# Fourteen convolution tiles of the last block as pairs of 64-row products

## The chip, the cores and the metric

The kernel runs on one core of a Trainium2 chip. The metric is the device time of one execution in microseconds (us). Engines are called TensorE (PE in the rows, PEld its weight loads), VectorE (DVE), ScalarE (ACT), GpSimd (POOL) and SyncE (SP, which issues most transfers). TensorE's clock has two levels, 1.2 and 2.4 GHz; the profile gives the granted clock as a share of the higher.

## The reference

Three blocks over a sequence of 1024 tokens of width 1024. The first two (windowed and dilated attention, each with a gated feed-forward part) are not touched. The change is in the third:

```python
xn = rmsnorm_2(h, norm_gain[l])
proj = jnp.einsum('bld,dc->blc', xn, w_in[l])
u_ssm, z_ssm = proj[..., :512], proj[..., 512:1024]
h_conv, b_conv, c_conv, z_conv = four slices of 512 columns
y_ssm = s5_mixer(u_ssm, ...) * jax.nn.silu(z_ssm)
y_conv = short_conv_mixer(h_conv, b_conv, c_conv, conv_w[l]) * jax.nn.silu(z_conv)
h = h + jnp.einsum('blc,cd->bld', concatenate([y_ssm, y_conv]), w_out[l])
```

with `short_conv_mixer(h, b, c, w) = b * sum(w[k] * shifted(c * h, k) for k in range(3))`. Everything is float32.

## The kernel before

**Products in three parts.** A float32 product is made of three fp32r products: with a value split into a high part (rounded to fp32r) and a low part (the rest), it is high x high, high x low and low x high. The activations are `hT_high` and `h_low_mix`, 128 rows x 8 chunks (k) x 1024 tokens. A convolution tile `("conv", j, w)` is 128 output columns: j is the block of 128 channels, w says which of the four slices (0 and 1 are multiplied with each other, 2 is the gate in front, 3 goes through silu). It takes 8 chunks x 3 parts x 2 halves of 512 tokens = 48 products of 128 rows x 512 columns in `split_products` (L1437), accumulated in one of four accumulators `acc[0]` to `acc[3]`, each of two banks of PSUM (one for each half of the tokens).

**Tiles and their order.** `CONVS` is the order of the 16 tiles: (0,0), (0,1), (0,2), (1,0), (0,3), (1,1), (1,2), (1,3), (2,0), ... (3,3). The first two are made together in `first_convs`. The other fourteen follow one by one in `project_h` or `project_around`. In between stand three pieces of other work: after (0,2) the column statistics (L2082, 32 products of one column, `("stats",)`, behind waits on `sum_a` and `sum_b`); inside (1,0), after 5 chunks, `factor_spread` (L2056, 16 products, `("r spread",)`); inside (1,1), after 4 chunks, `turn_c` (L2065, 4 transposes, `("c^T",)`). All three write to `acc[3]`. Then TensorE waits for `powers_ready` from GpSimd and goes on with `z_with_lags`, whose lag products (L2090) have 64 rows and use alternating row halves.

**Accumulators.** `CONV_PLACES` gives the accumulator of a tile. `take` waits until the last user's result has been read (`acc_free`), and a tile's last product raises `acc_ready`. A ledger (`plan_accumulators`) counts the uses.

**Weights.** Three slots in turn hold the tiles. SyncE loads tile n (512 KB, L882) when TensorE has ended tile n-3; ScalarE makes the high half (L2560, `tile_highs`), VectorE the low half (L3681, `tile_lows`), and `tile_of` on TensorE waits for the low half (`tile_split`).

**VectorE's order** is written out by hand. At the stage's start: the sums of the norm (fifteen instructions, L3866 to L3875), the low half of (1,0); the small steps from the statistics to the factor (L3886 to L3898), with the low half of (0,3) among them; the copy of the spread factor (L3900); then for j = 0 to 3 the convolution: the product with tile 1 (L3918), the taps (L3920, L3921) with one of them on ScalarE (L2820), the product with tile 2 (L3924), the product of tile 3 with the factor (L3926), L3929, silu on ScalarE (L2825), L3933. The low halves are put in between: for j = 0 that of (1,1) behind L3924 and that of (1,2) behind L3933. Then come, for j = 0 alone, the two copies of C transposed (L3939, L3940). For j = 1 the product of (1,0) (L3915) is next, then the low half of (1,3). From there the same pattern goes on: behind the reading of a tile, the low half of one three or more places later.

**GpSimd** works out powers for the state-space part: eight steps that wait for nothing late, then eight that begin with the copies of C transposed, and then a memset (L1387) that raises `powers_ready`.

Of the kernel before, what the change touches and what calls it, by code (L numbers as in the profile page):

```python
# [11 lines left out]
P = 128  # L12
D = 1024
S = 1024
KC = D // P
ST = S // P
HALF = 512
DH = 64
# [12 lines left out]
TB = 8  # L31
# [81 lines left out]
HIGH_FREED = {"S3": ("P5", 1), "A11": ("P2", 1), "A22": ("P3", 1), "S2": ("P6", 1), "S1": ("P7", 0), "A12": ("P1", 0), "S4": ("P4", 0)}  # L113
TAIL_PLACES = (2, 0, 1, 3, 2, 0, 3, 1)
LAST_PLACES = (2, 0, 3, 1, 2, 3, 0, 3)
CONV_PLACES = ((2, 1, 0, 3), (2, 1, 0, 3), (0, 1, 2, 3), (0, 1, 2, 3))
KEPT = ("P7", "P1", "P6")
FIRST_KEPT = ("P1", "P7", "P6")
ADDED = ("Y0", "Y1", "X0")
# [37 lines left out]
CONVS = [(j, w) for j in range(4) for w in range(4)]  # L157
# [171 lines left out]
def two_blocks_kernel(nc, x, x_rows, c, ada_tiles, columns, ffn_w_in, ffn_w_out, a_tiles, a_w_out, a_sink,  # L329
# [3 lines left out]
    ACC, WTS = plan_accumulators(), plan_weights()  # L333

    ctx = ExitStack()
    with ctx:
# [3 lines left out]
        def sem(name):  # L340
            return ctx.enter_context(nc.semaphore(name))
# [311 lines left out]
        ssm_power = sem("ssm_power")  # L653
        ssm_exp = sem("ssm_exp")
        inv_ready = sem("inv_ready")
        c_ready = sem("c_ready")
        powers_ready = sem("powers_ready")
        lag_zero = sem("lag_zero")
        lag_ready = sem("lag_ready")
# [457 lines left out]
        def _(pool):  # L1117
# [261 lines left out]
            for i in range(TB - 2, -1, -1):  # L1379
                cmul(bpow[:, 0, :, i, :], bpow[:, 1, :, i, :], bpow[:, 0, :, i + 1, :], bpow[:, 1, :, i + 1, :], turns(a_r, GC), turns(a_i, GC))  # L1380

            pool.wait_ge(c_ready, 1)
            pool.wait_ge(acc_free[3], ACC[("c^T",)][2] + 1)
            for j in range(TB):
                cmul(cpow[:, 0, :, j + 1, :], cpow[:, 1, :, j + 1, :], cpow[:, 0, :, j, :], cpow[:, 1, :, j, :], turns(a_r, GC), turns(a_i, GC), minus=True)
# [22 lines left out]
        def _(pe):  # L1408
            def take(name):

                d, number, freed = ACC[name]
                if freed:
                    pe.wait_ge(acc_free[d], freed)
                return acc[d], acc_ready[d]
# [605 lines left out]
            def project_h(name, wait=None):  # L2020

                dst, ready = take(name)
                high, low = tile_of(name, KC)
                split_products(dst, range(KC), lambda k: high[:, k, :], lambda k: low[:, k, :], lambda k: hT_high[:, k, :],
                               lambda k: h_low_mix[:, k, :], wait).then_inc(ready, 1)

            def first_convs():

                places = [take(("conv", 0, w)) for w in range(2)]
                pe.wait_ge(down_added, direct_number(1, STEPS - 1, 4))  # L2030
                tiles = [tuple(tile_of(("conv", 0, w), KC)) for w in range(2)]
                for k in range(KC):
                    pe.wait_ge(h2_ready, k + 1)
                    for (dst, ready), (high, low) in zip(places, tiles):
                        mm = split_products(dst, [k], lambda k: high[:, k, :], lambda k: low[:, k, :], lambda k: hT_high[:, k, :],
                                            lambda k: h_low_mix[:, k, :], None, k == 0, k == KC - 1)
                        if k == KC - 1:
                            mm.then_inc(ready, 1)

            def project_around(name, before, between):  # L2040

                dst, ready = take(name)
                high, low = tile_of(name, KC)
                for chunks in (range(before), range(before, KC)):
                    mm = split_products(dst, chunks, lambda k: high[:, k, :], lambda k: low[:, k, :], lambda k: hT_high[:, k, :],
                                        lambda k: h_low_mix[:, k, :], None, chunks[0] == 0, chunks[-1] == KC - 1)
                    if chunks[0] == 0:
                        between()
                mm.then_inc(ready, 1)
# [9 lines left out]
            def turn_c():  # L2059
# [5 lines left out]
                        mm = nc.tensor.transpose(dst[:, 256 * r + P * n:256 * r + P * n + P], c_raw[:, r, n, :], ident[:, :])  # L2065
                mm.then_inc(ready, 1)

            first_convs()
            for j, n in CONVS[2:]:
                if (j, n) == (1, 0):  # L2070
                    project_around(("conv", j, n), 5, factor_spread)
                elif (j, n) == (1, 1):
                    project_around(("conv", j, n), 4, turn_c)
                else:
                    project_h(("conv", j, n))
                if (j, n) == (0, 2):
                    dst, ready = take(("stats",))
                    pe.wait_ge(sum_a, KC - 1)
                    pe.wait_ge(sum_b, KC)
                    for a, sq in enumerate((squares_a[:, 1, :], squares_b[:, 1, :])):  # L2080
                        for i in range(TB):
                            mm = nc.tensor.matmul(dst[:, TB * a + i:TB * a + i + 1], sq[:, P * i:P * i + P], ones[:, :], start=True, stop=True)  # L2082
                    mm.then_inc(ready, 1)

            pe.wait_ge(powers_ready, 1)
            def lag_pair(d, k, r):

# [839 lines left out]
        def _(dve):  # L2927
# [978 lines left out]
            for j in range(4):  # L3906
                def tap(k):
                    at = CONV_W + 4 * k + j
                    return vec[:, at:at + 1]

                if j == 0:
                    copied(("conv", 0, 0))
                    after(nc.vector.tensor_tensor(conv_y, conv_y, r_squared, ALU.mult))
                else:
                    nc.vector.tensor_tensor(conv_y, ready(("conv", j, 0)), r_squared, ALU.mult).then_inc(free(("conv", j, 0)), 1)  # L3915
                    tile_lows(LAST_SPLITS[4 * j + 3])
                    copied(("conv", j, 0))
                nc.vector.tensor_tensor(conv_v[:, 2:2 + S], conv_y, ready(("conv", j, 1)), ALU.mult).then_inc(free(("conv", j, 1)), 1)  # L3918
                dve.wait_ge(conv_tap, j + 1)
                after(nc.vector.scalar_tensor_tensor(conv_y, conv_v[:, 1:1 + S], tap(1), conv_y, ALU.mult, ALU.add))  # L3920
                after(nc.vector.scalar_tensor_tensor(conv_y, conv_v[:, 2:2 + S], tap(2), conv_y, ALU.mult, ALU.add))  # L3921
                if j:
                    tile_lows(LAST_SPLITS[4 * j + 4])
                nc.vector.tensor_tensor(conv_y, conv_y, ready(("conv", j, 2)), ALU.mult).then_inc(free(("conv", j, 2)), 1)  # L3924
                tile_lows(LAST_SPLITS[4 * j + 5])
                nc.vector.tensor_tensor(conv_v[:, 2:2 + S], ready(("conv", j, 3)), r_tile, ALU.mult).then_inc(acc_free[3], 1)  # L3926
                copied(("conv", j, 3))
                copied(("conv", j, 2))
                after(nc.vector.tensor_tensor(conv_y, conv_y, r_tile, ALU.mult))  # L3929
                dve.wait_ge(conv_silu, j + 1)  # L3930
                if j == 2:
                    dve.wait_ge(b_read, 1)
                nc.vector.tensor_tensor(y_conv[:, j, :], conv_y, conv_v[:, 2:2 + S], ALU.mult).then_inc(conv_ready, 1)  # L3933
                tile_lows(LAST_SPLITS[4 * j + 6])
                dve.wait_ge(conv_ready, j + 1)
                if j == 0:

                    c_rows = ready(("c^T",))[:, 0:512].rearrange("p (r c h) -> p r c h", r=2, c=NP)
                    nc.vector.tensor_copy(cpow[:, 0, :, 0, :], c_rows[:, 0]).then_inc(c_ready, 1)  # L3939
                    nc.vector.tensor_scalar(cpow[:, 1, :, 0, :], c_rows[:, 1], -1.0, None, ALU.mult).then_inc(acc_free[3], 1)  # L3940

            dve.wait_ge(conv_ready, 4)
# [195 lines left out]
```

## Time and profile before

| | |
|---|---|
| median of 3 runs | 2556.8 us (2555.84 to 2558.6) |
| the profiled execution | 2559.55 us |
| its span, first to last instruction | 2557.8 us |
| mean granted clock of TensorE | 0.997 |
| TensorE busy | 2519.9 us, 99% |
| VectorE busy | 1979.4 us, 77% |

All times in rows are from the span's start. A row of the timeline merges equal instructions that follow each other: start, length, engine, line, operation, output<-input, shape, count, and in brackets the idle time before it with what ended it. Products overlap in the array, so a row of n products is n-1 steps and one product's length long.

### The profile page before, as it was taken

To read this page: it belongs to the slowest core of one execution; us is meant where nothing else is said; L and a number is where in the kernel's file an instruction comes from. 1 tells how busy PE (TensorE), PEld (TensorE's weight loads), DVE (VectorE), ACT (ScalarE), POOL (GpSimd) and SP (SyncE) were. 2 spreads that over 40 slices of the span, in tenths; PEclk is the share of its full clock that TensorE was granted. 3 is DMA by queue.
4 is the path that set the end of the run, shared out by engine and by line. 5 is a ranking of instruction groups with operands and counts; after the bars stand their busy time and mean duration, and the time that the engine had idled before them with its cause. 6 is when DMAs were issued, how large, how long until landed. Compare 5 with 4: busy or idle time off the path is not lost.

```text
span 2557.8 us, 37284 instructions
## 1 busy us (share of the span) xinstructions
PE 2519.9 (99%) x12662; PEld 2042.5 (80%) x12662; DVE 1979.4 (77%) x3476; ACT 1071.7 (42%) x2010; POOL 318.0 (12%) x454
## 2 busy tenths in 40 slices
PE   8999999999999999999999999999999999999998
PEld 6777688888888888777776888888888888878987
DVE  7899848889998898845555898989999987443566
ACT  6666725433333333454445443333333342111233
POOL 2011101000000000201111200000000018971000
PEclk9999999999999999999999999999999999999999
DMA  6334231211112111222332111111112131113122
GB/s 240 121 135 141 100 91 58 65 59 49 53 53 62 53 53 53 105 69 91 99 108 92 50 50 46 59 60 49 53 57 62 49 101 57 50 42 60 34 99 83
DMA packets 182019, 192.62 MB, mean 75 GB/s; under 512 B 18354, under 2 KB 146578, under 8 KB 181491
## 3 DMA queue, kind: packets, MB, share of 16 engines
q1 hardware_dynamic: 169954, 147.48, 18.1%
q0 software_dynamic: 11952, 43.65, 5.5%
q8 instruction: 69, 1.13, 0.2%
q14 instruction: 44, 0.35, 0.0%
HBM read 177.34 MB, written 12.58 MB: 74 GB/s over the span
## 4 chain that ended last, share of the span: by engine, by line
PE 93%; DVE 3%; ACT 2%; issue 1%; DMA 0%; POOL 0%; SPq 0%; DVEq 0%
PE psum L1437 21%; PE psum L1759 10%; PE psum L1761 10%; PE psum L1760 10%; PE psum L1514 5%; PE psum L1811 4%; PE psum L1815 4%; PE psum L1812 4%; PE psum L1516 4%; PE psum L1515 4%; PE psum L1800 3%; PE psum L1645 3%; PE psum L1629 3%; PE psum L1614 1%; DVE arena L2955 1%; PE psum L1610 1%
## 5 line engine op out<-in xcount | busy, mean ns | idle before, releaser
L3244 DVE SCALAR_TENSOR_TENSOR xT<-psum,mod,xT 128x512 f32<-128x512 f32 x504 | 356.7, 747 | 61.5 <-PE psum L1815 61.2
L2375 ACT ACTIVATE w_high<-wpair 128x512 fp32r<-128x512 f32 x240 | 146.4, 626 | 315.7 <-DVE wpair L3176 244.5
L1437 PE MATMUL psum<-hT_high,w_low 128*128 128x512 f32 x928 | 263.1, 394 | 0.2 <-DVE arena L2951 0.2
L1437 PEld LDWEIGHTS psum<-hT_high,w_low 128*128 128x128 f32 x928 | 174.3, 189 | 38.6 <-issue 2.5
L1514 PE MATMUL psum<-hT_high,w_low 128*128 128x512 f32 x480 | 200.2, 417 | 3.4 <-DVE h_low_mix L3719 3.3
L2593 ACT ACTIVATE arena<-arena 128x256 f32<-128x256 f32 (+3 forms) x296 | 146.6, 498 | 118.3 <-DVE arena L3530 118.0
L1516 PE MATMUL psum<-hT_high,w_low 128*128 128x512 f32 x480 | 189.0, 394 | 0.0
L1515 PE MATMUL psum<-h_low_mix,w_low 128*128 128x512 f32 x480 | 188.6, 393 | 0.0
L1761 PE MATMUL psum<-hT_high,w_low 128*128 128x512 f32 x480 | 186.7, 389 | 0.0
L1759 PE MATMUL psum<-hT_high,w_high 128*128 128x512 f32 x472 | 183.6, 389 | 0.0
L1760 PE MATMUL psum<-h_low,w_high 128*128 128x512 f32 x472 | 183.6, 389 | 0.0
L3162 DVE TENSOR_TENSOR w_low<-wpair,w_high 128x512 fp32r<-128x512 f32 x240 | 162.2, 683 | 2.4 <-ACT w_high L2375 1.9
L3681 DVE TENSOR_TENSOR w_low<-wpair,w_low 128x1024 fp32r<-128x1024 f32 x70 | 89.4, 1278 | 88.9 <-ACT w_low L2560 88.6
L1237 POOL TENSOR_TENSOR w_high<-arena,w_high 128x512 fp32r<-128x512 f32 x2 | 2.6, 1290 | 1233.5 <-ACT w_high L2362 1233.5
L1811 PE MATMUL psum<-hT_high,w_low 128*128 128x512 f32 x360 | 140.0, 389 | 0.0
L1437 PE MATMUL psum<-h_low_mix,w_low 128*128 128x512 f32 x448 | 136.2, 393 | 0.2 <-ACT arena L2302 0.2
L2560 ACT ACTIVATE w_low<-wpair 128x1024 fp32r<-128x1024 f32 x76 | 80.0, 1054 | 130.1 <-DMA wpair<-in_w_in_dram 94.6
L1514 PEld LDWEIGHTS psum<-hT_high,w_low 128*128 128x128 f32 x480 | 90.3, 188 | 44.5 <-issue 24.7
L3530 DVE CUSTOM_DVE_ANT_0 arena<-psum,arena 128x192 f32<-128x192 f32 (+2 forms) x180 | 53.7, 353 | 86.6 <-PE psum L1614 86.6
L2421 ACT ACTIVATE arena<-psum 128x512 f32<-128x512 f32 x80 | 47.9, 599 | 169.9 <-PE psum L1761 114.3
L2614 ACT ACTIVATE arena<-psum 128x1024 f32<-128x1024 f32 (+2 forms) x80 | 85.4, 1067 | 75.5 <-PE psum L1629 75.1
L3176 DVE TENSOR_TENSOR wpair<-wpair 128x512 f32<-128x512 f32 x160 | 110.0, 688 | 6.6
(492 smaller groups left out, 6362.4 us busy)
## 6 DMA issues: line engine op xcount, KB each, us to landing
wpair<-in_ffn_w_in_dram SPq DMA_DIRECT2D x176, 256.0 KB, 2.9
wpair<-in_ada_tiles_dram POOLq DMA_DIRECT2D x20, 1024.0 KB, 5.3
arena<-in_ffn_w_out_dram SPq DMA_DIRECT2D x80, 256.0 KB, 2.9
wpair<-in_ada_tiles_dram POOLq DMA_DIRECT2D x32, 512.0 KB, 3.6
wpair<-in_w_in_dram SPq DMA_DIRECT2D x24, 512.0 KB, 3.8
wpair<-in_b_tiles_dram SPq DMA_DIRECT2D x18, 512.0 KB, 3.3
arena<-in_ada_tiles_dram SPq DMA_DIRECT2D x8, 1024.0 KB, 15.8
wpair<-in_a_tiles_dram SPq DMA_DIRECT2D x12, 512.0 KB, 5.1
```

The lines of the kernel that those rows point to most:

```text
L1437: mm = nc.tensor.matmul(dst[:, HALF * a:HALF * a + HALF], w(k), src(k)[:, HALF * t:HALF * t + HALF], start=first and n == 0 and w is high ...
L1514: nc.tensor.matmul(dst, high[:, k, :], hT_high[:, k, rows], start=k == 0, stop=False)
L1515: nc.tensor.matmul(dst, high[:, k, :], h_low_mix[:, k, rows], start=False, stop=False)
L1516: mm = nc.tensor.matmul(dst, low[:, k, :], hT_high[:, k, rows], start=False, stop=k == KC - 1)
L1759: nc.tensor.matmul(bank[dst], high[:, k, :], moving_high(k), start=start and k == 0, stop=False, skip_group_check=not start)
L1760: nc.tensor.matmul(bank[dst], high[:, k, :], moving_low(k), start=False, stop=False, skip_group_check=not start)
L1761: mm = nc.tensor.matmul(bank[dst], low[:, k, :], moving_high(k), start=False, stop=k == 3, skip_group_check=not start)
L1811: nc.tensor.matmul(dst, down_high[w][:, cols], hid_high[v], start=start, stop=False, skip_group_check=not start)
L2375: nc.scalar.activation(of_step(s, first_high, part_high)[name], part_raw[name], ACT.Copy).then_inc(part_high_ready, 1)
L2593: e = nc.scalar.activation(s, s, ACT.Exp, bias=stat_n[:, ti, h:h + 1], scale=-1.0, accum_out=stat_l[:, ti, h:h + 1])
L3162: nc.vector.tensor_tensor(part_low[name], part_raw[name], as_f32(high), ALU.subtract).then_inc(part_split, 1)
L3244: nc.vector.scalar_tensor_tensor(xT[:, m, rows], psum[:, HALF * j:HALF * j + HALF], mod[:, l, 40 + m:41 + m], xT[:, m, rows], ALU.mult, AL ...
```

## The change

Products of the fourteen tiles behind `first_convs` are cut into products of 64 rows. `by_rows` makes one pass over a tile: for each chunk and part, the upper 64 rows are multiplied for one half of the tokens and the lower 64 rows for the other half, so the two go to two banks. A second pass (`swapped`) exchanges the halves and adds what is missing. A pass is 24 such pairs. Two tiles are made together in `pair_of_tiles`: first pass of tile A, first pass of tile B, second pass of A (behind a wait on the new semaphore `rows_done`, raised by A's first pass), second pass of B (likewise). The pairs are (0,2) with (1,0), (0,3) with (1,1), (1,2) with (1,3), and so on. The column statistics stand behind the first passes of the first pair, `factor_spread` inside its last pass after 5 chunks, `turn_c` behind the first pass of (1,2). The places of the tiles of j = 2 and 3 are those of j = 0 and 1. `c_ready` goes, and `inv_ready` counts to 2 in its place. VectorE's, ScalarE's and SyncE's orders are otherwise as before.

```diff
-CONV_PLACES = ((2, 1, 0, 3), (2, 1, 0, 3), (0, 1, 2, 3), (0, 1, 2, 3))
+CONV_PLACES = ((2, 1, 0, 3), (2, 1, 0, 3), (2, 1, 0, 3), (2, 1, 0, 3))
...
-            pool.wait_ge(c_ready, 1)
+            pool.wait_ge(inv_ready, 2)
...
+            def by_rows(name, swapped, chunks=range(KC)):
+
+                d = ACC[name][0]
+                high, low = tile_of(name, KC)
+                for k in chunks:
+                    for w, srcs in ((high, (hT_high, h_low_mix)), (low, (hT_high,))):
+                        for s in srcs:
+                            first, last = k == 0 and w is high and s is hT_high, k == KC - 1 and w is low
+                            for row in (0, DH):
+                                half = int(row > 0) ^ int(swapped)
+                                at, rows = slice(HALF * half, HALF * half + HALF), slice(row, row + DH)
+                                mm = nc.tensor.matmul(acc[d][:, at], w[rows, k, :], s[rows, k, at], start=first and not swapped, stop=last and swapped)
+                if KC - 1 in chunks:
+                    mm.then_inc(acc_ready[d] if swapped else rows_done, 1)
+
+            def pair_of_tiles(i, names, behind_first=None, behind_firsts=None, inside_last=None):
+
+                take(names[0])
+                by_rows(names[0], False)
+                if behind_first:
+                    behind_first()
+                take(names[1])
+                by_rows(names[1], False)
+                if behind_firsts:
+                    behind_firsts()
+                pe.wait_ge(rows_done, 2 * i + 1)
+                by_rows(names[0], True)
+                pe.wait_ge(rows_done, 2 * i + 2)
+                by_rows(names[1], True, range(5))
+                if inside_last:
+                    inside_last()
+                by_rows(names[1], True, range(5, KC))
...
             first_convs()
-            for j, n in CONVS[2:]:
-                if (j, n) == (1, 0):
-                    project_around(("conv", j, n), 5, factor_spread)
-                elif (j, n) == (1, 1):
-                    project_around(("conv", j, n), 4, turn_c)
-                else:
-                    project_h(("conv", j, n))
-                if (j, n) == (0, 2):
...
+            pairs = [[("conv", j, w) for j, w in CONVS[n:n + 2]] for n in range(2, 16, 2)]
+            pair_of_tiles(0, pairs[0], None, column_statistics, factor_spread)
+            pair_of_tiles(1, pairs[1])
+            pair_of_tiles(2, pairs[2], turn_c)
+            for i in range(3, 7):
+                pair_of_tiles(i, pairs[i])
             pe.wait_ge(powers_ready, 1)
...
-                    nc.vector.tensor_copy(cpow[:, 0, :, 0, :], c_rows[:, 0]).then_inc(c_ready, 1)
+                    nc.vector.tensor_copy(cpow[:, 0, :, 0, :], c_rows[:, 0]).then_inc(inv_ready, 1)
```

## Rows read from the trace of the kernel before

**Rows 1.** The page: span, busy times, clock by slices, chain that ended last.
```profile
span 2557.8 us, 37284 instructions
...
PE 2519.9 (99%) x12662; PEld 2042.5 (80%) x12662; DVE 1979.4 (77%) x3476; ACT 1071.7 (42%) x2010; POOL 318.0 (12%) x454
...
PEclk9999999999999999999999999999999999999999
...
PE 93%; DVE 3%; ACT 2%; issue 1%; DMA 0%; POOL 0%; SPq 0%; DVEq 0%
```

**Rows 2.** The chain from 2120 to 2290: start, us, what, count.
```profile
2119.94 17.91 PE psum L1437 x79
2137.84 3.82 PE psum L2082 x32
2141.66 9.76 PE psum L1437 x30
2151.43 1.78 PE psum L2056 x16
2153.21 20.44 PE psum L1437 x90
```

**Rows 3.** Windows: length, busy time and count by engine, granted clock, DMA.
```profile
core 0: us, PE busy (x) PEld busy (x) DVE busy (x) ACT busy (x) POOL busy (x), PEclk, DMA share, GB/s
...
2141.50:2147.60 6.10, 6.10 (x15) 4.79 (x16) 3.72 (x17) 0.42 (x2) 4.80 (x17) 0.50 0.00 0
...
27.90:31.30 3.40, 3.40 (x10) 2.62 (x9) 3.37 (x7) 0.82 (x2) 0.00 (x0) 0.51 1.02 408
```

**Rows 4.** TensorE's timeline, ahead of the second of these windows.
```profile
27.01 0.50 PE L1514 MATMUL psum<-hT_high,w_low 128*128 128x512 f32 x1 [2.55 <-DVE h_low_mix L3719]
```

**Rows 5.** TensorE's timeline: plain fp32 products, of 64 and of 128 rows.
```profile
1127.03 1.13 PE L1614 MATMUL psum<-arena 64*128 64x256 f32 x8
...
2423.49 3.73 PE L2178 MATMUL psum<-arena,hT 128*128 128x128 f32 x32
...
2441.03 3.98 PE L2187 MATMUL psum<-arena 64*128 64x128 f32 x64
```

**Rows 6.** TensorE's timeline around the first lag products.
```profile
2289.13 0.61 PE L1437 MATMUL psum<-hT_high,w_low 128*128 128x512 f32 x2
2289.67 0.61 PE L2090 MATMUL psum<-arena 64*16 64x128 f32 x8
2290.22 0.73 PE L1437 MATMUL psum<-hT_high,w_low 128*128 128x512 f32 x2
```

**Rows 7.** VectorE's timeline, from the norm's sums to tile (1,2).
```profile
2133.95 2.03 DVE L3873 TENSOR_TENSOR arena<-arena 128x1024 f32<-128x1024 f32 x1
2135.82 1.22 DVE L3681 TENSOR_TENSOR w_low<-wpair,w_low 128x1024 fp32r<-128x1024 f32 x1
...
2146.01 0.17 DVE L3898 TENSOR_TENSOR r_token<-rst 128x8 f32<-128x8 f32 x1
...
2153.25 2.19 DVE L3900 COPY arena<-psum 128x1024 f32<-128x1024 f32 x1 [7.08 <-PE psum L2056]
...
2164.38 1.56 DVE L3681 TENSOR_TENSOR w_low<-wpair,w_low 128x1024 fp32r<-128x1024 f32 x1
2168.25 1.23 DVE L3926 TENSOR_TENSOR arena<-psum,arena 128x1024 f32<-128x1024 f32 x1 [2.30 <-PE psum L1437]
...
2172.43 1.64 DVE L3681 TENSOR_TENSOR w_low<-wpair,w_low 128x1024 fp32r<-128x1024 f32 x1
```

**Rows 8.** The copies of C, what follows them on VectorE; GpSimd's last step.
```profile
2174.20 0.42 DVE L3939 COPY arena<-psum 128x256 f32<-128x256 f32 x1
...
2176.00 1.22 DVE L3681 TENSOR_TENSOR w_low<-wpair,w_low 128x1024 fp32r<-128x1024 f32 x1
...
2243.79 0.11 POOL L1387 MEMSET arena<- 128x16 f32 x1
```

**Rows 9.** VectorE's timeline from a tile's end to the next split; the load.
```profile
2190.50 1.22 DVE L3924 TENSOR_TENSOR arena<-arena,psum 128x1024 f32<-128x1024 f32 x1 [3.95 <-PE psum L1437]
2195.31 1.56 DVE L3681 TENSOR_TENSOR w_low<-wpair,w_low 128x1024 fp32r<-128x1024 f32 x1 [3.58 <-ACT w_low L2560]
...
wpair<-in_w_in_dram SPq DMA_DIRECT2D x11, 512.0 KB, 3.8
```

More of the change, by code:

```diff
@@ L655, in two_blocks_kernel @@
         inv_ready = sem("inv_ready")
-        c_ready = sem("c_ready")
+        rows_done = sem("rows_done")
         powers_ready = sem("powers_ready")
@@ L2066, in turn_c @@
                 mm.then_inc(ready, 1)
-            first_convs()
-            for j, n in CONVS[2:]:
-                if (j, n) == (1, 0):
-                    project_around(("conv", j, n), 5, factor_spread)
-                elif (j, n) == (1, 1):
-                    project_around(("conv", j, n), 4, turn_c)
-                else:
-                    project_h(("conv", j, n))
-                if (j, n) == (0, 2):
[L2077 to L2083, printed above, removed]
+            def by_rows(name, swapped, chunks=range(KC)):
[11 more added lines that the diff above has]
+                    mm.then_inc(acc_ready[d] if swapped else rows_done, 1)
@@ new lines, in column_statistics @@
+            def column_statistics():
+                dst, ready = take(("stats",))
+                pe.wait_ge(sum_a, KC - 1)
+                pe.wait_ge(sum_b, KC)
+                for a, sq in enumerate((squares_a[:, 1, :], squares_b[:, 1, :])):
+                    for i in range(TB):
+                        mm = nc.tensor.matmul(dst[:, TB * a + i:TB * a + i + 1], sq[:, P * i:P * i + P], ones[:, :], start=True, stop=True)
+                mm.then_inc(ready, 1)
+            first_convs()
+            pairs = [[("conv", j, w) for j, w in CONVS[n:n + 2]] for n in range(2, 16, 2)]
```

## The prediction

> **What bounds the kernel now.** I read the page first. TensorE is busy 2519.9 of 2557.8 us and carries 93% of the chain that ended last; its granted clock is at the higher level (2.4 GHz) in nearly every slice [rows 1]. So the program ends when TensorE's queue has been worked off, and a change of this stage is worth what it adds to or takes from that queue. The chain over the stage shows the stage's make-up: 79, 30 and 90 products in a row, broken only by the column statistics and the spread of a factor, with no wait of TensorE between them [rows 2]. The last of these pieces gives the rate: 20.44 us for 90 products of 128x512 is 0.2271 us each; I use 0.2267, which the single timeline steps repeat. The tile (0,2) begins 48 products before the statistics, at 2137.68 - 48 x 0.2267 = 2126.80.
>
> Next the windows, for the clock. The statistics are 32 products of one column, 3.8 us [rows 2]; just after them the granted clock is 0.50 for 6.1 us, that is 1.2 GHz [rows 3]. There 30 products take 9.76 us [rows 2] instead of 6.8: 3.0 us lost. A second place shows the same after real idleness: TensorE waits 2.55 us [rows 4] and the next 3.4 us run at 0.51 [rows 3], 1.7 us lost. An idle stretch of a few us on TensorE thus costs itself and a further 1.7 to 3.0 us.
>
> Last the DVE queue, in order of time, because DVE makes the low half of each weight tile (L3681), and TensorE can't start a tile before it.
>
> **The change, part by part.**
>
> *Products.* 14 tiles x 48 = 672 full products become 672 pairs of 64-row products, each pair into two banks. The trace has 64-row products in alternating row halves and banks, but in plain fp32, whose columns take twice as long. Attention's, 256 columns (8 in 1.13 us, the first lasting 0.48): three further pairs in 0.65 us, 0.217 a pair [rows 5], for what is 512 column times, 0.2133 us at 2.4 GHz; some 3 ns on top. The full fp32r product has 13.4 ns on top of the same 0.2133. With 128 columns, 64 products of 64 rows take 3.98 us, 0.124 a pair with the first one's latency in it and 0.117 without, against 3.73/32 = 0.117 for a full 128-row product [rows 5]. So pairs do run side by side, at least level with a full product. Bounds for a pair here: 0.216 and 0.2267. I take 0.216, as attention's rows are the nearest in stream length (512 column times a pair) and way of issue: 672 x 0.0107 = -7.2 us. At the other end the gain is nothing.
>
> *Changes between 128-row and 64-row products.* Around the lag products, the step 2289.36 to 2289.67 is 0.31 instead of 0.23, and 2289.67 to 2290.22 is 0.55 for four pairs of 0.11: some 0.2 us for a way in and out [rows 6]. The stage has four such: the whole, and the statistics, spread and turn of C inside it. +0.8 us. The Trainium skill, "TensorEngine Tiling (Array Packing)", Key Properties, says that a change of tiling mode drains the engine; these rows agree.
>
> *First stall: tile (1,0).* Before, TensorE wants it after all 48 products of (0,2) and after the statistics, past 2141. Now its first pass comes after 24 pairs, at 2126.8 + 0.1 + 24 x 0.216 = 2132.1. Its low half is the DVE instruction at 2135.82, ended 2137.04 [rows 7], behind the fifteen sums of the norm, which DVE has worked through without a gap; nothing of them moves. Stall 5.0 us.
>
> *Second stall: tile (1,1).* Its low half lies on DVE behind a chain that begins with the spread of the factor: from 2153.25 to 2164.38 + 1.56 = 2165.94, 12.7 us [rows 7]. Before, TensorE had 18 products of (1,0) and 48 of (0,3) left after the spread, 15.0 us: the tile was ready 2.3 us before it was wanted. Now it has 9 pairs of (1,0) and one pass of 24 of (0,3): 7.1 us, plus some 0.4 for the bank of (0,3), which the copy of 2.19 us frees [rows 7]. Stall 12.7 - 7.1 - 0.4 = 5.2, and 0.4 before it. The factor itself isn't late: its last step stands 4.5 us behind the statistics' end [rows 7], and 39 pairs lie between.
>
> *Third: tile (1,2).* DVE takes (0,3) at 2168.25, when TensorE ends it, and has the low half of (1,2) at 2172.43 + 1.64 = 2174.07 [rows 7], 5.8 us. Between the end of (0,3) and the start of (1,2) there is now one pass, 5.2 us. Stall 0.6, with semaphore steps 0.8.
>
> *Fourth: C transposed.* The transposes move from inside (1,1) to behind the first pass of (1,2). DVE waits for them in its fixed order, and behind that wait stand the two copies, the product of (1,0) and the low half of (1,3): 2174.20 to 2177.22, 3.0 us [rows 8]. TensorE needs that low half for its very next pass. With the transposes' own latency: stall 3.4 us. GpSimd, which waits for the same copies, has its powers ready at 2243.79 [rows 8], 44 us before TensorE asks for them (the next stage begins six products before 2289.67 [rows 6], at 2288.2); the 24 us that C comes late are covered. The new semaphore count (2 in place of a semaphore of its own) costs nothing.
>
> *From the fourth pair on.* A slot freed by the first of a pair must be filled again within two passes, 10.4 us. The row pattern gives 2190.50 (tile done) to 2195.31 + 1.56 = 2196.87 (split done), 6.4 us, the load's 3.8 us in it [rows 9]: no stall, 4 us to spare. The bank orders leave each bank at least a pass to be read. The waits on rows_done look at a pass that ended a whole pass earlier: nothing.
>
> *Clock.* The first, second and fourth stall are longer than the 2.55 us after which the clock fell [rows 3, 4]. Each costs 1.7 to 3.0 us; I take 2.4, three times, +7.0 us. The statistics cost their 3.0 us before and after. The Trainium skill, "TensorE: Matmul & The Clock Gate", HAM oscillation, also has idle gaps of a few us bring the lower clock back; the rows agree.
>
> **Sum.** Stalls 5.0 + 0.4 + 5.2 + 0.8 + 3.4 = 14.8; clock 7.0; switches 0.8; pairs -7.2: +15.4 us. The profiled execution took 2559.55 us (span 2557.8), so 2575.0 for it. It stands 2.75 above the median of the three runs, 2556.8; against the median 2572.2. Predicted: 2572 us.
>
> **Rivals.**
> (a) A pair costs what the full product costs, 0.2267, as the rows with 128 columns say [rows 5]; against it stands attention's 3 ns. The stalls hardly change (4.7 the first), so +22.6: 2579.4. The Trainium skill, "TensorEngine Tiling (Array Packing)", Overview, promises gain from row tiling only where the contracted dimension is small; here it is a whole 128, and by that rule this is the case.
> (b) The pair is slower than a full product: the two weight changes are paid one after the other, 0.2133 + 2 x 0.0134 = 0.240 us, +9.0 instead of -7.2: 2588. If the two products did not overlap at all, 0.43 us a pair, it would be some 140 us more; the 64-row rows speak against that.
> (c) The stalls come, but the clock stays up after them, since each is soon followed by dense products: +8.4, 2565.2. Against it: the fall after 2.55 us.
> (d) Not slower. Mechanism: the pairs stream faster than one column a cycle and row half. To pay 14.8 + 7.0 + 0.8 = 22.6 us, 672 pairs must each save 33.6 ns, so it decides at 0.193 us a pair. That is under the 0.2133 that 512 columns need, and no row shows it.
>
> **How the numbers follow.** Forecast 0.50, (a) 0.27, (b) 0.08, (c) 0.11, (d) 0.04. The range: from (c), 2565, to (a) with 3.0 us of clock at each stall, 2556.8 + 14.8 + 9.0 + 0.8 = 2581.4, rounded up for pairs a little above 0.2267: 2564 to 2583. It leaves out (b) and (d), 12 in 100. The runs before lie within 0.1% of each other, so 0.2% (5 us) is about what can be told from no change. Faster: only (d), of which half, 0.02; same the other half, 0.02; slower 0.96.
>
> **What would show it.** TensorE idle some 5 us from about 2132, released by DVE L3681; again some 5 us in the middle of the pair (0,3), (1,1); 3 to 4 us behind the transposes of C; granted clock at 0.5 after each. Starts of pairs 0.216 apart (0.227 for (a), 0.240 for (b)). From the fourth pair on no idleness. The stage, 2126.8 to 2288.2 before, ends near 2304. It would be wrong if DVE came to the low half of (1,0) before 2132, or if the pair's rate were not between 0.216 and 0.227.

## The result and the profile after

The changed kernel takes 2583.14 us (median of four runs, 2582.84 to 2583.51), the kernel before 2557.7 (2555.84 to 2558.96): 1.0% slower, ratio 1.0100, 95% interval 1.0087 to 1.0113. The forecast was 2572, with a range of 2564 to 2583: right in direction, too low by 11 us, and 0.14 us outside the range. The profiled executions are 2582.84 and 2559.55 us, 23.3 apart.

The page of the changed kernel, against [rows 1]:

```profile
span 2581.1 us, 38642 instructions
...
PE 2528.2 (98%) x13334; PEld 2063.4 (80%) x13334; DVE 1979.3 (77%) x3476; ACT 1073.1 (42%) x2010; POOL 314.0 (12%) x454
...
PEclk9999999999999999999999999999999998999999
```

TensorE has 672 product records more and is busy 8.3 us longer (a part of it at the lower clock); the other 15 of the 23.3 us are idle time. The chain through the stage, against [rows 2], shows where it went:

```profile
2136.23 1.06 DVE w_low L3714
...
2137.43 7.32 PE psum L2079 x47
2144.75 3.94 PE psum L2108 x32
2148.69 11.97 PE psum L2079 x73
2160.66 2.00 PE psum L2056 x16
...
2162.68 2.20 DVE arena L3933
...
2174.46 1.47 DVE w_low L3714
...
2176.07 14.02 PE psum L2079 x96
...
2194.31 1.70 DVE w_low L3714
...
2196.14 5.75 PE psum L2079 x48
2201.89 0.60 PE psum L2065 x4
...
2204.47 1.33 DVE w_low L3714
...
2205.94 105.27 PE psum L2079 x912
```

Before, this stretch of the chain was TensorE alone. Now it leaves TensorE four times for VectorE, and each time it comes back through L3714, the low half of a tile (L3681 before). The same four waits in TensorE's timeline, with the idle time in brackets:

```profile
2137.43 0.56 PE L2079 MATMUL psum<-hT_high,w_low 64*128 64x512 f32 x2 [4.33 <-DVE w_low L3714]
...
2176.07 0.80 PE L2079 MATMUL psum<-hT_high,w_low 64*128 64x512 f32 x2 [5.39 <-DVE w_low L3714]
...
2196.14 0.49 PE L2079 MATMUL psum<-hT_high,w_low 64*128 64x512 f32 x2 [0.63 <-DVE w_low L3714]
...
2205.94 0.77 PE L2079 MATMUL psum<-hT_high,w_low 64*128 64x512 f32 x2 [3.46 <-DVE w_low L3714]
```

They are the first passes of (1,0), (1,1), (1,2) and (1,3). A record lasts 0.39 us and the next would begin 0.227 after its start, so each costs 0.16 us more than its bracket: 4.5, 5.6, 0.8 and 3.6, together 14.5 us. Behind three of them the clock is down, as these windows show (granted clock is the first number behind POOL's):

```profile
2137.43:2144.70 7.27, 7.27 (x49) 6.25 (x49) 0.01 (x1) 0.00 (x0) 5.44 (x23) 0.77 0.01 2
...
2148.60:2154.80 6.20, 6.20 (x31) 4.88 (x33) 3.83 (x17) 0.42 (x2) 5.43 (x23) 0.50 0.00 0
2176.07:2182.10 6.03, 6.03 (x28) 5.22 (x30) 0.00 (x0) 0.00 (x0) 5.79 (x10) 0.50 0.00 0
...
2205.90:2209.40 3.50, 3.46 (x16) 3.25 (x18) 2.28 (x2) 2.10 (x2) 3.34 (x5) 0.51 0.03 5
2209.40:2311.00 101.60, 101.60 (x898) 98.64 (x894) 38.63 (x28) 13.73 (x13) 73.80 (x94) 1.00 0.17 48
```

The second is the statistics' own, as before. In the first the clock comes back up before the pass is over, so its mean is 0.77. From 2209.4 on TensorE is never idle and the clock is up, and a pair takes 0.2267 us from start to start (mean of 444 steps), which is the step of a full product. That is rival (a).

VectorE's side, against [rows 7] and [rows 8]: the low half of (1,0) is made when it was before, that of (1,1) 13.2 us behind the spread (12.7 before), and the copies of C wait 6.6 us for TensorE.

```profile
2136.07 1.21 DVE L3714 TENSOR_TENSOR w_low<-wpair,w_low 128x1024 fp32r<-128x1024 f32 x1
...
2162.68 2.19 DVE L3933 COPY arena<-psum 128x1024 f32<-128x1024 f32 x1 [9.37 <-PE psum L2056]
...
2174.38 1.54 DVE L3714 TENSOR_TENSOR w_low<-wpair,w_low 128x1024 fp32r<-128x1024 f32 x1
...
2202.58 0.42 DVE L3972 COPY arena<-psum 128x256 f32<-128x256 f32 x1 [6.59 <-PE psum L2065]
```

A measure for what follows: **the stage**, from the start of the last feed-forward product (L1800) to the start of the first lag product (L2090 before, L2123 after). It is 184.86 us before (2104.81 to 2289.67) and 207.47 after (2105.26 to 2312.73): +22.6. The part ahead of it differs by up to 3.7 us between executions in which nothing of it was changed (2104.8 to 2108.5), so single spans can't tell a microsecond here, and the stage can.

### The profile page after: what moved, and what is told of

Its sections match the earlier page's. It is cut to its first block, busy times and chain, and to the rows that moved or that the text cites. A ratio compares the mean times of both kernels' runs of the same rounds, so it can differ in the third digit from the quotient of the medians.

```text
span 2581.1 us, 38642 instructions
## 1 busy us (share of the span) xinstructions
PE 2528.2 (98%) x13334; PEld 2063.4 (80%) x13334; DVE 1979.3 (77%) x3476; ACT 1073.1 (42%) x2010; POOL 314.0 (12%) x454
## 3 DMA queue, kind: packets, MB, share of 16 engines
q1 hardware_dynamic: 169954, 147.48, 17.7%
## 4 chain that ended last, share of the span: by engine, by line
PE 91%; DVE 5%; ACT 2%; issue 1%; DMA 0%; POOL 0%; SPq 0%; DVEq 0%; ACTq 0%
PE psum L1437 14%; PE psum L1759 10%; PE psum L1760 10%; PE psum L1761 10%; PE psum L2079 6%; PE psum L1514 5%; PE psum L1812 4%; PE psum L1815 4%; PE psum L1811 4%; PE psum L1516 4%; PE psum L1515 4%; PE psum L1645 3%; PE psum L1629 3%; PE psum L1800 2%; PE psum L1614 1%; DVE arena L2988 1%
## 5 line engine op out<-in xcount | busy, mean ns | idle before, releaser
L1514 PE MATMUL psum<-hT_high,w_low 128*128 128x512 f32 x480 | 200.7, 418 | 3.0 <-DVE h_low_mix L3752 2.8
L1516 PE MATMUL psum<-hT_high,w_low 128*128 128x512 f32 x480 | 189.1, 394 | 0.0
L1515 PE MATMUL psum<-h_low_mix,w_low 128*128 128x512 f32 x480 | 188.8, 393 | 0.0
L1761 PE MATMUL psum<-hT_high,w_low 128*128 128x512 f32 x480 | 186.7, 389 | 0.0
L2079 PE MATMUL psum<-hT_high,w_low 64*128 64x512 f32 x896 | 152.8, 403 | 13.8 <-DVE w_low L3714 13.8
L3714 DVE TENSOR_TENSOR w_low<-wpair,w_low 128x1024 fp32r<-128x1024 f32 x70 | 89.0, 1272 | 83.3 <-ACT w_low L2593 83.0
L1437 PE MATMUL psum<-hT_high,w_low 128*128 128x512 f32 x480 | 140.8, 394 | 0.2 <-DVE arena L2984 0.2
L1811 PE MATMUL psum<-hT_high,w_low 128*128 128x512 f32 x360 | 140.1, 389 | 0.0
L1514 PEld LDWEIGHTS psum<-hT_high,w_low 128*128 128x128 f32 x480 | 90.6, 189 | 44.0 <-issue 24.7
L2079 PEld LDWEIGHTS psum<-hT_high,w_low 64*128 64x128 f32 x896 | 100.5, 194 | 23.4 <-issue 15.6
## 6 DMA issues: line engine op xcount, KB each, us to landing
arena<-in_ada_tiles_dram SPq DMA_DIRECT2D x8, 1024.0 KB, 15.6
```

The costliest lines, as they stand in the source:

```text
L1437: mm = nc.tensor.matmul(dst[:, HALF * a:HALF * a + HALF], w(k), src(k)[:, HALF * t:HALF * t + HALF], start=first and n == 0 and w is high ...
L1514: nc.tensor.matmul(dst, high[:, k, :], hT_high[:, k, rows], start=k == 0, stop=False)
L1515: nc.tensor.matmul(dst, high[:, k, :], h_low_mix[:, k, rows], start=False, stop=False)
L1516: mm = nc.tensor.matmul(dst, low[:, k, :], hT_high[:, k, rows], start=False, stop=k == KC - 1)
L1761: mm = nc.tensor.matmul(bank[dst], low[:, k, :], moving_high(k), start=False, stop=k == 3, skip_group_check=not start)
L1811: nc.tensor.matmul(dst, down_high[w][:, cols], hid_high[v], start=start, stop=False, skip_group_check=not start)
```

## The experiments

The theory: the pairs cost what full products cost, and the 22.6 us are three late low halves and a short fourth (14.5), the clock behind them, and under 1 us for changes between 128 and 64 rows. The rivals: 64-row products are themselves the slow part; or the stalls are one chain, where what one gives back another takes.

| kernel | median us | ratio (95%) | stage us | stage to before |
|---|---|---|---|---|
| changed | 2583.14 | 1.0100 (1.0087 to 1.0113) | 207.47 | +22.6 |
| e1, full products, new order | 2583.04 | 1.0092 (1.0077 to 1.0108) | 206.76 | +21.9 |
| e2, 64 rows, old order | 2567.02 | 1.0027 (1.0017 to 1.0038) | 189.69 | +4.8 |
| e3, three moves | 2562.47 | 1.001 (1.0001 to 1.0019) | 185.20 | +0.3 |
| e5, low half of (1,0) earlier | 2577.51 | 1.0067 (1.0053 to 1.008) | 199.63 | +14.8 |
| e6, low half of (1,1) earlier | 2577.18 | 1.0063 (1.0049 to 1.0076) | 198.85 | +14.0 |
| e7, C transposed earlier | 2578.03 | 1.007 (1.0056 to 1.0084) | 200.54 | +15.7 |
| e8, e3 with full products | 2559.87 | 1.0003 (0.9994 to 1.0012) | 184.56 | -0.3 |
| e9, statistics between products | 2559.42 | 0.9995 (0.9986 to 1.0004) | 182.48 | -2.4 |
| e10, stalls filled | 2576.64 | 1.0071 (1.0058 to 1.0085) | 200.42 | +15.6 |

The kernel before had medians of 2560.18 (beside e1 to e4), 2560.75 (e5, e6, e7, e9) and 2558.91 us (e8, e10); the ratios are to those. Each stage is read from one profiled execution. The expectations below give the distance from the kernel before without saying by which measure; where medians and stages disagree about them, the text says so.

### e1: full products in the new order

```diff
-                            for row in (0, DH):
-                                half = int(row > 0) ^ int(swapped)
-                                at, rows = slice(HALF * half, HALF * half + HALF), slice(row, row + DH)
-                                mm = nc.tensor.matmul(acc[d][:, at], w[rows, k, :], s[rows, k, at], ...)
+                            at = slice(HALF * int(swapped), HALF * int(swapped) + HALF)
+                            mm = nc.tensor.matmul(acc[d][:, at], w[:, k, :], s[:, k, at], start=first, stop=last)
```

> The order of the changed kernel (pairs of tiles, four passes, statistics, spread and turn where the change puts them), but each pass made of 24 full products of 128 rows for one half of the tokens. Theory (the time comes from the order: three late low halves and the clock behind them; a pair of 64-row products costs what one full product does): stalls of 4.5, 5.4, 0.6 and 3.5 us and the fallen clock stay; only the changes between 128 and 64 rows go, so 0.5 to 1.5 us below the changed kernel, 21 to 25 us above the kernel before, ratio 1.008 to 1.010. Rival (64-row products are what is slow): within 5 us of the kernel before.

21.9 of the 22.6 us stay without a single 64-row product in the fourteen tiles. The waits are those of the changed kernel, four for the low half and 0.2 us for the bank of (0,3):

```profile
PE psum L2077 <- DVE w_low L3712: 14.4, 4, 5.7
PE psum L2077 <- DVE arena L3931: 0.2, 1, 0.2
```

So the order is what costs. The difference left for the 64 rows is 0.7 us. It is what they add on balance: e1 waits longer, 14.4 us for low halves against 13.8 in the changed kernel, and 0.2 for the bank, which TensorE's waits in the changed kernel do not show. So a part of what the 64 rows cost is hidden behind waits that are there anyway; the rows themselves may cost up to 0.7 + 0.6 + 0.2 = 1.5 us, an estimate.

### e2: 64-row products in the old order

```diff
-            pairs = ...
-            pair_of_tiles(...)
+            for n in range(2, 16):      # one tile at a time
+                take(name); by_rows(name, False)
+                pe.wait_ge(rows_done, n - 1)
+                by_rows(name, True)
```

(The spread stands in the second pass of (1,0) after 2 chunks, C transposed between the passes of (1,1); the accumulators' places are those of before.)

> 64-row products in the order of the kernel before: one tile at a time, its first pass, the wait on rows_done, its second pass; statistics, spread and turn after as many products as before. Theory: no stall by a low half, the clock as before; 0.8 us for the changes between 128 and 64 rows, and at each of 14 swaps the wait for the first pass's last product, worked out at 0.25 us from a product's 0.39 us in the records against a step of 0.227: 3.5 us. 3 to 6 us above the kernel before, ratio 1.001 to 1.0025. Rival (64-row products are what is slow): 20 us or more above.

The stage is 4.8 us longer than before, in the forecast 3 to 6. The chain of the kernel, one tile to a row:

```profile
2199.36 11.22 PE psum L2079 x96
2210.58 0.04 issue
2210.62 11.22 PE psum L2079 x96
```

A tile takes 11.26 us against 48 x 0.2267 = 10.88: 0.38 for the wait at the swap, where I had worked out 0.25, and 14 x 0.38 = 5.3. That is what making two tiles together avoids, and it is less than what the order of the pairs cost. The stage met its forecast with help: behind the statistics the clock cost 1.85 us here and 2.9 in the kernel before (see e3), so at an equal clock the stage would be some 6 us longer, which is 5.3 and the 0.8 for changes of rows. The median is 6.8 us above before, ratio 1.0027, and that is a miss of the expected 3 to 6 us and 1.001 to 1.0025; the part ahead of the stage was 2.2 us longer in the profiled execution.

### e3: the three moves

```diff
 # VectorE, norm's sums
                 weighted(k, ...)
+                if k == KC - 2:
+                    tile_lows(LAST_SPLITS[3])
                 plain(k, ...)
 # VectorE, convolution, j == 0 (ScalarE's high half likewise ahead of its tap)
+                    tile_lows(LAST_SPLITS[5])
                 dve.wait_ge(conv_tap, j + 1)
 # TensorE
-            pair_of_tiles(1, pairs[1])
-            pair_of_tiles(2, pairs[2], turn_c)
+            pair_of_tiles(1, pairs[1], None, None, turn_c)
+            pair_of_tiles(2, pairs[2])
```

> The changed kernel with three moves: the low half of (1,0) put before the last but three of the norm's sums; the high and low half of (1,1) put before the first tap; C transposed inside the last pass of the second pair, after 5 chunks. Theory: the stalls of 4.5, 5.4 and 3.5 us and their clock (1.6, 2.8, 1.6 us) go, some 19.5 us; left over are the changes between 128 and 64 rows and stalls under 1 us each: 1 to 4 us above the kernel before, ratio 1.0003 to 1.0015. Rival (64-row products are what is slow): still 15 us or more above.

The stage is 22.3 us shorter than the changed kernel's and 0.3 us longer than before's, under the expected 1 to 4 us; the median is 2.3 us longer, within them. The chain stays on TensorE from end to end:

```profile
2129.21 11.15 PE psum L2079 x96
2140.36 3.66 PE psum L2108 x32
2144.02 10.69 PE psum L2079 x78
2154.71 1.98 PE psum L2056 x16
2156.69 2.30 PE psum L2079 x18
...
2159.00 20.01 PE psum L2079 x174
2179.01 0.59 PE psum L2065 x4
2179.60 111.13 PE psum L2079 x975
```

A part of this may not be the moves' doing: behind the statistics 39 pairs take 10.69 us, 1.85 more than their 8.84 at the higher clock, where the changed kernel loses 3.1 (11.97) and the kernel before 2.9. The loss is as small, 1.6 to 1.9 us, in e2, e5, e7, e8 and e10, but not in e1 (2.9) and e6 (2.65). e7 pays for it elsewhere: its first stall is there, and the pass behind that stall takes 8.34 us, against 7.32 in the changed kernel.

```profile
2139.76 8.34 PE psum L2079 x48
2148.10 3.66 PE psum L2108 x32
2151.76 10.69 PE psum L2079 x75
```

What sets how long the clock stays down is not settled. Some 1.3 us of e3's gain on the changed kernel, and 1.1 us of how well it compares with the kernel before, hang on it and are not shown to come from the moves.

### e5, e6, e7: each move alone

> The changed kernel with the low half of (1,0) alone put before the last but three of the norm's sums. Theory: each stall stands for itself and costs its idle time and half of the time at the fallen clock behind it; here 4.5 and 1.6 us go, the stalls before (1,1), (1,2) and (1,3) stay at 5.4, 0.6 and 3.5 us: 16 to 18 us above the kernel before, ratio 1.006 to 1.007. Rival (one chain: what the first stall gives back is lost again at the second): still 20 us or more above.

> The changed kernel with the high and low half of (1,1) alone put before the first tap. Theory: 5.4 us of stall and 2.8 us of clock go, less some 0.3 us: 14 to 16 us above the kernel before, ratio 1.0055 to 1.0065. Rival (the chain behind it, with one instruction more ahead of the taps, makes the wait before (1,2) longer and takes half of it back): 18 us or more above.

> The changed kernel with C transposed inside the last pass of the second pair, after 5 chunks, and nothing else. Theory: VectorE then has the copies behind it when it comes to (1,0) and the low half of (1,3) before TensorE asks; 3.5 us of stall and 1.6 us of clock go, 17 to 19 us above the kernel before, ratio 1.0065 to 1.0075. Rival (VectorE would be late with the low half of (1,3) anyway, as the slot of (0,3) is only then loaded anew): less than 2 us gained on the changed kernel.

Each is faster than the changed kernel by more than a wait: 7.8, 8.6 and 6.9 us of stage. Taken by the starts of passes in the traces, e5 gains 7.7 us up to the spread, 1.5 of them at the statistics and behind them; e6 gains 8.3 around (1,1) and nothing at the statistics, whose own 32 records take 0.5 us longer while the pairs behind them lose 0.5 less; e7 gains 6.6 from (1,1) on. Elsewhere each differs from the changed kernel by 0.6 us at most. The three pieces add up to 22.6, and e3 gained 22.3: the stalls add up. The rival of one chain falls. So does that of e7, where VectorE was said to be late anyway. e7's 6.6 are its stall of 3.5, its clock of 1.6, the wait before (1,2) of 0.8, which went with it, and 0.5 less clock lost behind the stall of (1,1), for which no cause is shown.

The ratios came out as expected in all three. The medians are 16.8, 16.4 and 17.3 us above before, the second 0.4 over its range. The stages, at +14.8, +14.0 and +15.7, are 1.2 and 1.3 us under the ranges of e5 and e7, and at the lower end of that of e6. e5's other three waits stand as they were:

```profile
PE psum L2079 <- DVE w_low L3714: 9.4, 3, 5.0
```

### e8: the moves with full products

The edit is e1's and e3's together.

> The three moves of e3 and full products in place of 64-row pairs, in the new order. Theory: against e3 only the changes between 128 and 64 rows go, 0.7 us as between the changed kernel and e1; level with the kernel before, ratio 1.000, the stage within 1 us of before's 184.9 us from the last feed-forward product to the first lag product. Rival (the new order costs something of its own besides the three stalls): 2 us or more above the kernel before in the stage.

0.6 us below e3 in the stage and 0.3 below before, as expected. That does not make the new order free. The clock behind the statistics costs 1.6 us here and 2.9 in the kernel before, so at an equal clock e8 would be some 1 us above. TensorE's waits show where a part of it lies, in the bank of (0,3) and the low half of (1,2):

```profile
PE psum L2077 <- DVE w_low L3711: 0.4, 1, 0.4
PE psum L2077 <- DVE arena L3931: 0.2, 1, 0.2
```

e3 has no such wait, so the 0.6 us between e3 and e8, as the 0.7 between the changed kernel and e1, is what 64 rows cost on balance, and not all that they cost.

### e10: stalls filled with products that nobody uses

```diff
-                take(names[1])
+                dst, _ = take(names[1])
+                if i < 3:
+                    spare_products((10, 12, 6)[i], dst[:, 0:256])
                 by_rows(names[1], False)
```

> The changed kernel with spare products put where it stalls: 10, 12 and 6 products of 256 columns in plain fp32 (two records each, 0.43 us a product) into the accumulator of (1,0), (1,1) and (1,3) ahead of the tile's own first pass. They compute nothing that is used. Theory (1.6, 2.8 and 1.6 us of the change's time are the clock that falls because TensorE was idle): the low halves come no sooner, but the clock stays at 1 behind all three; 5 to 6 us less than the changed kernel in the stage, less some 0.6 us for the changes of mode, 16 to 19 us above the kernel before, ratio 1.0065 to 1.0075. Rival (the clock falls by something else, or costs less than worked out): within 2 us of the changed kernel, or above it by what the spare products add.

The low halves come as late as ever, but the stage falls by 7.0 us, more than the expected 5 to 6; 1.3 of them are clock behind the statistics. The median, 17.7 us above before, is in its range, and the stage at +15.6 is just under it. Granted clock in the first two filled stalls and behind each of them, and behind the third:

```profile
2133.50:2138.00 4.50, 4.50 (x24) 3.70 (x22) 4.41 (x4) 1.61 (x2) 4.26 (x4) 1.00 0.00 0
2138.00:2143.00 5.00, 5.00 (x45) 4.10 (x46) 0.00 (x0) 0.00 (x0) 3.70 (x16) 1.00 0.01 3
2168.00:2173.50 5.50, 5.50 (x28) 4.53 (x26) 5.17 (x4) 2.26 (x3) 5.42 (x5) 1.00 0.00 0
2173.50:2179.50 6.00, 6.00 (x55) 4.95 (x56) 0.00 (x0) 0.00 (x0) 5.76 (x10) 1.00 0.01 3
...
2201.00:2206.50 5.50, 5.50 (x48) 4.51 (x50) 4.21 (x4) 2.10 (x2) 5.34 (x6) 1.00 0.00 0
```

1.00 throughout, where the changed kernel had 0.77, 0.50 and 0.51. So the fallen clock behind the stalls is a consequence of TensorE's idleness, and it is worth the 5.7 us left over.

### e4: the disputed cost by itself

Products were added at the end of the kernel before, 32 (or 32 pairs) of each width in turn, the whole series twice, whole (L2296 fp32r, L2300 plain fp32) and as 64-row pairs (L2305, L2310).

> The kernel before with runs of 32 products (or pairs) added at its very end, behind the last result of TensorE, into a free accumulator; the output is untouched by them and the time is longer by them. Whole and 64-row pairs, fp32r with 512, 384 and 256 columns, plain fp32 with 512, 256 and 128. Theory A (the 13 ns beyond the columns' own time belong to fp32r products, whatever the rows; each row half has them for itself): fp32r whole and pair alike, 0.2267, 0.173, 0.120 us; plain records 0.43, 0.216 for both. Theory B (the gap belongs to 128-row products): pairs of fp32r 0.216, 0.163, 0.109. Theory C (each of a pair pays it): 0.240, 0.187, 0.133.

```profile
2553.02 16.94 PE L2296 MATMUL psum<-hT_high 128*128 128x512 f32 x96
2569.89 16.94 PE L2305 MATMUL psum<-hT_high 64*128 64x512 f32 x192
2586.76 48.69 PE L2300 MATMUL psum<-hT_high 128*128 128x512 f32 x192
2635.38 48.70 PE L2310 MATMUL psum<-hT_high 64*128 64x512 f32 x384
```

It was run once, and only the rows at its end are read. Each row holds three widths; the second series repeats all four lengths. 96 whole fp32r products and 96 pairs take the same 16.94 us; the plain ones, 48.69 and 48.70. By starts, fp32r takes 0.227, 0.174 and 0.120 us for 512, 384 and 256 columns, whole or paired: 13 to 14 ns beyond a column per cycle at 2.4 GHz. Plain records take 0.429, 0.216 and 0.112 for 512, 256 and 128, whole or paired: 2 cycles a column and 2 to 5 ns. Theory A.

### e9: a version faster than before?

In the kernel before, `project_around` for (1,0) is replaced: the statistics go behind its first three chunks (12, 10 and 10 records), the spread behind the sixth.

```diff
+                for k in range(KC):
+                    mm = split_products(dst, [k], ...)
+                    if k < 3:
+                        for a, i in (left[0:6], left[6:11], left[11:16])[k]:
+                            st = nc.tensor.matmul(sums[:, ...], sq[:, ...], ones[:, :], start=True, stop=True)
+                    if k == 2:
+                        st.then_inc(sums_ready, 1)
+                    if k == 5:
+                        factor_spread()
```

> The kernel before, with full products in its own order, but the 32 products of one column of the statistics put between the products of (1,0): 12, 10 and 10 behind its first three chunks, and the spread behind the sixth. Theory (the clock falls when TensorE does next to nothing for some microseconds, idle or with such tiny products): the granted clock stays at 1, the 3.0 us lost behind the statistics come back, less some 0.4 us for a later spread: 2 to 3 us below the kernel before, ratio 0.999. Rival (the clock answers to something else there): it falls as before, within 1 us of the kernel before.

```profile
2141.60:2149.00 7.40, 7.40 (x50) 6.67 (x50) 0.24 (x2) 0.17 (x1) 5.49 (x24) 1.00 0.25 73
2148.00:2153.00 5.00, 4.75 (x23) 3.65 (x22) 3.69 (x17) 0.42 (x2) 4.06 (x16) 1.00 0.00 0
```

The same tiny products, between dense ones, leave the clock up in this trace, where it was 0.50 before [rows 3]. The stage is 2.4 us shorter than before's, as expected. In the medians it is 1.3 us, less than the expected 2 to 3, and the interval of the ratio (0.9986 to 1.0004) includes no change: seen in one trace, not shown by the timing. It is the best of all kernels here by its stage.

## Why the prediction came out too low

**The step that failed** is "I take 0.216 ... 672 x 0.0107 = -7.2 us", the product term. Measured: a pair takes 0.2267, the term is nil. I had both ends and took the wrong row. Attention's pairs have 3 ns beyond their columns because they are plain fp32, not because they are 64 rows: e4 finds the same 2 to 5 ns for whole plain records and the same 13 to 14 for fp32r pairs. The nearest row in type was missing, and the 128-column rows [rows 5], where a pair took what a whole product does, were the better witness. (a) had 0.27. Its +22.6 is the stage's +22.6, but that is in part luck: it was summed with the stalls for 0.216; at 0.2267 the forecast's own rows give 4.7, 0.4, 4.8, 0.6 and 3.4, and with 7.2 for the clock and the 0.8 the sum is 21.9. The Trainium skill, "TensorEngine Tiling (Array Packing)", Overview, which the prediction set beside (a), counts a contract dimension of at most 64 among the cases in which the full array is underused. The runs agree: a contracted dimension of 128, cut in two, gained nothing (16.94 us either way in e4).

**The stalls**, 14.8 us worked out, are 14.5: 4.5 (5.0 forecast; 4.7 for (a)), 5.6 (5.2), 0.8 (0.8), 3.6 (3.4), each at the tile, behind the instruction and in the order named. For the bank of (0,3), forecast 0.4, the changed kernel's list of waits has 0.4 on the weight load's side and e1's 0.2.

**The clock**, 7.0 us forecast, is 5.7 by e10. By the passes in the trace it is 7.25 - 5.71 (the same pass in e10) = 1.5 behind the first stall, some 2.8 behind the second and 1.6 behind the fourth, 5.9 in all. Each stretch is between the 1.7 and 3.0 that the two rows of before gave, or just under. (Three times the 2.4 of the forecast are 7.2; it wrote 7.0.)

**Changes between 128 and 64 rows**, 0.8 us forecast, are 0.6 to 0.7 on balance by e1 and e8, and perhaps up to 1.5 by themselves, as e1's longer waits say.

**Covered things** were covered: no stall from the fourth pair on, none on GpSimd's powers, none on `rows_done` (e2 shows what it costs where nothing lies between: 0.38 us a tile).

With 0 for -7.2 the sum is +22.6; with what was measured, 14.5 + 0.2 + 5.9 + 0.7 = 21.3, and 1.3 us of the stage stay unassigned; the 0.8 us by which the changes of rows may cost more than 0.7 would be a part of them. The miss of 10.9 us between the forecast of 2572.2 and the median of 2583.14 is made up of the 7.2 of this term, 0.9 by which the median of the kernel before rose with its fourth run (2556.8 to 2557.7), and 2.8 by which the medians' difference, 25.4 us, is above 22.6. The profiled executions are 23.3 us apart; the interval (22 to 29 us) holds both, and no run settles these 2.8 us. With the term at 0 the forecast would have been 2557.7 + 22.6 = 2580.3, within the range, which ended 0.14 us short of the measured median. That it ended at the high end of (a) and gave slower pairs 0.08 was thin for a value whose place between its bounds rested on rows of another type.

Slips of reading: the statistics are 16 products in the kernel's code and the spread is 8, which a plain fp32 product's two records turn into 32 and 16 rows; and of the 64-row products in [rows 5] two records make one product likewise. None of these changed a term, but they should have warned that these are not the products of the change.

## What to carry to other kernels

Halving the rows of full 128-row products gained nothing here. The two passes of a tile want another tile's pass between them (e2), and it was the new order that cost. Before tiles are interleaved, list for each when its operands are ready and when it is now wanted: the first pass of the second tile of a pair moves forward by half a tile, and the instruction that feeds it must move with it on the other engine's queue. Once each did, here, 22 us came back (e3).

An idle stretch of 3.6 to 5.6 us on TensorE cost a further 1.5 to 2.8 us here through the clock. Where it can't be removed, spare products in it gave that part back (e10). Tiny products put between dense ones instead of in one block kept the clock up in e9's trace; the whole time does not confirm the gain.

Where a cost is bounded by rows of another data type, keep both ends in the forecast; the type may be what the difference is about.

## What the runs showed of the hardware that I had not expected

- The gap of 13 to 14 ns on top of one column per cycle goes with fp32r, at 512, 384 and 256 columns, and each row half has it for itself: two 64-row products in alternating halves run side by side, and 96 pairs take as long as 96 whole products (16.94 us).
- Behind the same statistics the clock cost different amounts in different kernels: 3.1 us in the changed kernel, 2.9 in the kernel before, 1.85 in e3, 1.6 in e8. Such a difference can hide or feign a gain of 1 us.
- TensorE's clock also fell behind a block of 32 records of one column, with no idle time in the records at all (0.50 behind 3.8 us of them [rows 3]), and did not fall with the same records spread over three chunks (e9).
